# Delta-net inversion with two heads beside each other in one 128-column product, and 16 of 32 modulation row products moved to the first attention

## The reference, cut to what matters

```python
mod = jax.nn.silu(c) @ w_ada[layer] + b_ada[layer]            # 6 x 1024 numbers
sh1, sc1, gt1, sh2, sc2, gt2 = jnp.split(mod, 6, axis=-1)
A = where(strict, einsum('id,jd->ij', kb, kc) * decay, 0.0)   # for a chunk and head
t_inv = triangular_solve(A + eye, eye, lower=True, unit_diagonal=True)
W = t_inv @ (kb * exp(Gcum));  U = t_inv @ (vc * bc)
v_new = U - W @ S;  S = S * gt + kt.T @ v_new                 # from chunk to chunk
```

## Time and profile before

| what | us |
|---|---|
| runs | 1801.17, 1801.20, 1801.35; median 1801.2 |
| span of the profiled execution | 1798.0 |
| outside the span, against the median | 3.2 |
| first attention, tiles 23 on | about 149 to 244 |
| inversion, first product to the end of the last level's updates | 255.05 to 403.4 |
| apply of the last round, read-out and norm up to the second phase's end | to 419.5 |

### The profile page before, as it was taken

The page is one execution under the profiler, slowest core; times in us unless marked ns, Lnnn a source line. Parts: engine busy times, 40 slices in busy tenths (PEclk is TensorE's granted clock), DMA queues, the critical chain, the costliest instruction groups (busy, mean ns, idle before and its releaser), DMA issues.

```text
span 1798.0 us, 34944 instructions
## 1 busy us (share of the span) xinstructions
PE 1751.7 (97%) x11968; PEld 1581.6 (88%) x11968; DVE 1300.8 (72%) x2596; ACT 1053.4 (59%) x2118; POOL 163.3 (9%) x136
## 2 busy tenths in 40 slices
PE   7999999999999999999999999999999999999998
PEld 1878789999999988888899999999899899999997
DVE  3787456667889979766766666666686767878887
ACT  2545553343666689766655555555657666766666
POOL 0000004410284420000000000000010000010000
PEclk9999999999999999999999999999999999999999
DMA  8433223234455421355555555555444534455553
GB/s 298 183 105 106 80 86 114 75 105 170 149 197 175 166 93 37 117 193 191 189 197 186 187 187 186 187 186 187 152 176 142 198 130 141 165 181 186 184 186 129
DMA packets 77273, 283.34 MB, mean 158 GB/s; under 512 B 8576, under 2 KB 8576, under 8 KB 76928
## 3 DMA queue, kind: packets, MB, share of 16 engines
q1 hardware_dynamic: 77184, 282.16, 45.6%
HBM read 281.08 MB, written 1.05 MB: 157 GB/s over the span
## 4 chain that ended last, share of the span: by engine, by line
PE 83%; DVE 10%; ACT 4%; issue 1%; POOL 1%; DMA 1%; PEld 0%; PEldq 0%; ACTq 0%; SPq 0%; DVEq 0%
PE banks L867 19%; PE banks L855 16%; PE banks L946 10%; PE banks L455 7%; PE banks L1102 7%; PE banks L1126 3%; PE banks L646 2%; PE banks L797 2%; PE banks L627 2%; DVE split L2331 2%; DVE arena L2327 2%; PE banks L423 1%; PE banks L635 1%; PE banks L960 1%; PE banks L1062 1%
## 5 line engine op out<-in xcount | busy, mean ns | idle before, releaser
L1447 ACT ACTIVATE split<-arena 128x512 fp32r<-128x512 f32 x492 | 309.0, 629 | 135.1 <-PE banks L855 76.9
L855 PEld LDWEIGHTS banks<-split 128*128 128x128 f32 x2880 | 355.4, 192 | 10.6 <-DVE split L2257 3.1
L867 PE MATMUL banks<-split 128*128 128x512 f32 x1536 | 361.9, 390 | 1.0 <-issue 1.0
L855 PE MATMUL banks<-split 128*128 128x256 f32 x2880 | 358.7, 283 | 3.2 <-DVE split L2257 2.3
L2349 DVE TENSOR_TENSOR split<-arena,split 128x512 fp32r<-128x512 f32 x396 | 270.7, 690 | 105.5 <-ACT split L1447 99.7
L867 PEld LDWEIGHTS banks<-split 128*128 128x128 f32 x1536 | 283.8, 188 | 57.3 <-issue 1.4
L1425 ACT ACTIVATE split<-arena 128x512 fp32r<-128x512 f32 x312 | 194.5, 627 | 112.1 <-PE banks L1102 52.8
L946 PE MATMUL banks<-split 128*128 128x256 f32 x1728 | 216.8, 287 | 4.3 <-DVE split L2427 3.9
L946 PEld LDWEIGHTS banks<-split 128*128 128x128 f32 x1728 | 211.9, 194 | 7.2 <-issue 6.0
L2404 DVE TENSOR_TENSOR split<-arena,split 128x512 fp32r<-128x512 f32 x180 | 123.1, 694 | 65.3 <-ACT split L1425 63.8
L455 PEld LDWEIGHTS banks<-split 128*128 128x128 f32 (+1 forms) x936 | 132.4, 192 | 28.5 <-issue 13.8
(11 more groups left out here) (412 smaller groups left out, 2418.2 us busy)
## 6 DMA issues: line engine op xcount, KB each, us to landing
arena<-wstream SPq DMA_DIRECT2D x525, 512.0 KB, 3.3
arena<-x_t SPq DMA_DIRECT2D x1, 2048.0 KB, 12.4
arena<-matsa SPq DMA_DIRECT2D x1, 1234.0 KB, 6.3
out_t<-arena SPq DMA_DIRECT2D x4, 256.0 KB, 2.0
arena<-mats SPq DMA_DIRECT2D x1, 576.0 KB, 8.1
arena<-crow SPq DMA_DIRECT2D x1, 512.0 KB, 7.1
arena<-rows SPq DMA_DIRECT2D x1, 512.0 KB, 4.1
arena<-mats SPq DMA_DIRECT2D x1, 449.0 KB, 4.2
```

The source lines that it names most:

```text
L855: mm = pe.matmul(ps[:, 4 + b, 0:S], w_parts[:, c, (2 * m + half) % 4, P * k:P * k + P], h_parts[:, e, 4 * half + k, :], start=(half == 0 a ...
L867: mm = pe.matmul(ps[:, 2 * tt + half, :], g_parts[:, e, j % 2, P * tt:P * tt + P], w_parts[:, c, (2 * m + half) % 4, :], start=(first and ...
L1447: act.activation(w_parts[:, 0, (2 * m + half) % 4, :], ring[:, peer_slot(m), 512 * half:512 * half + 512], ACT.Copy).then_inc(sem["w_hi"], 1)
```

## The change

It packs the half of `Z` that a level works on, and the keys it needs, so that two heads lie side by side in one 128x128 block. One product with 128 columns then serves two heads; what comes out between different heads is zeroed by a mask of blocks (`blocks`), in place of the mask of a single head. So each level has two products, two turns and two products of 128 columns for each direction. ACT gets new work: `pack_keys` gathers the keys of the next level, `keep_half` carries over the half of `Z` that a level doesn't change, and at level 6 it copies the products in two pieces. `Z` alternates between `Z1` and `Z2`, so the products wait for DVE's subtraction and for both ACT copies. The copy of `T` halves to 128x256. `first_inverse` becomes two DVE instructions of 128x256.

16 of the 32 `mod_tail` now stand in the first attention, each behind `both_lo` of a tile (the first two behind tiles 23 and 24), and their weight tiles alternate with tiles 23 to 38 in `wstream` and in the ring. 2 stay before the inversion and 14 within it. Two waits (`gain3_in`, `lam_exp`) go.

```diff
@@ -44,6 +44,9 @@
...
+FIRST_TAIL, EARLY_TAILS = 23, 16
+in_at = lambda t: N_WIN + t + min(max(t - FIRST_TAIL, 0), EARLY_TAILS)
+tail_at = lambda a: N_WIN + FIRST_TAIL + 2 * a + 1 if a < EARLY_TAILS else N_ADA2 + a
@@ -233,9 +236,9 @@
...
         at = buf("at", 4, 4, P)
-        PAIR = ("E", "A0", "A1", "Z0", "Z1", "T", "KB", "VB", "KT", "S", "wt", "uu")
-        pair = [{n: buf(f"{n}{d}", 4, P) for n in PAIR} for d in range(2)]
-        yp = [buf(f"yp{d}", 256) for d in range(2)]
+        PAIR = ("E", "A0", "A1", "Z0", "Z1", "Z2", "AP", "T", "KB", "VB", "KT", "S", "wt", "uu")
+        pair = [{n: buf(f"{n}{d}", 2 if n == "T" else 4, P) for n in PAIR} for d in range(2)]
@@ -326,7 +329,35 @@
...
+        flat = lambda v: v.rearrange("p a b -> p (a b)")
         parts = lambda v, l, q: v.rearrange("p (b q s) -> p b q s", q=2, s=2 ** l)[:, :, q, :]
+        def inverse_at(d, l):
+            return flat(pair[d]["Z0" if l == 1 else "Z1" if l % 2 == 0 else "Z2"])
+        def half_at(d, l, q):
+            return inverse_at(d, l)[:, 256 * q:256 * q + 256]
+        def next_half(d, l, q):
+            v = inverse_at(d, l + 1)
+            if l == 6:
+                return parts(v, 6, q)
+            return v.rearrange("p (x g q s) -> p x g q s", x=2, q=2, s=2 ** l)[:, :, :, q, :].rearrange("p x g s -> p g x s")
+        def as_next(v, l):
+            return v.rearrange("p (g s) -> p g s", s=64) if l == 6 else v.rearrange("p (g x s) -> p g x s", x=2, s=2 ** l)
+        def as_packed(v, l):
+            return v.rearrange("p (g s) -> p g s", s=2 ** l)
+        def keys_at(d, l):
+            return flat(pair[d]["AP"])[:, 256 * (l % 2):256 * (l % 2) + 256]
         block = ctx.enter_context(nc.Block())
@@ -363,16 +394,21 @@
...
-                    sp.wait_ge(sem["in_lo"], 2 * (n - RING - N_WIN) + 2)
+                    if n - RING in in_tiles:
+                        sp.wait_ge(sem["in_lo"], 2 * in_tiles[n - RING] + 2)
+                    else:
+                        sp.wait_ge(sem["tail_done"], early_tails[n - RING] + 1)
                     sp.dma_start(tile_at(n), wstream[n]).then_inc(loaded[n % RING], 16)
+            in_tiles = {in_at(t): t for t in range(39)}
+            early_tails = {tail_at(a): a for a in range(EARLY_TAILS)}
@@ -616,40 +652,38 @@
                 mm.then_inc(sem["m_turned"], 1)
             def level_products(n, l, d):
-                z, a = pair[d][f"Z{n % 2}"], pair[d][f"A{n % 2}"]
                 if l == 1:
                     if n == 0 and d == 1:
                         pe.wait_ge(sem["proj_free"], 4 + 39)
                     pe.wait_ge(sem["z1_ready"], step_at(n, d))
                 else:
                     pe.wait_ge(sem["z_ready"], level_at(n, l - 1, d))
-                for h in range(4):
-                    mm = pe.matmul(ps[:, d, 64 * h:64 * h + 64], a[:, h, :], parts(z[:, h, :], l, 1 - d), start=True, stop=True)
+                    pe.wait_ge(sem["z_kept"], level_at(n, l - 1, d))
+                pe.wait_ge(sem["keys_packed"], level_at(n, l, d))
+                for j in range(2):
+                    c = slice(P * j, P * j + P)
+                    mm = pe.matmul(ps[:, d, c], keys_at(d, l)[:, c], half_at(d, l, 1 - d)[:, c], start=True, stop=True)
                 mm.then_inc(sem["y_done"], 1)
                 if l == 1:
                     if n:
                         pe.wait_ge(sem["wu_ready"], step_at(n - 1, d))
                     else:
                         pe.wait_ge(sem["tok_ready"], 3 + d)
-                for h in range(4):
-                    mm = pe.transpose(ps[:, 2 + d, P * h:P * h + P], z[:, h, :], ident)
+                for j in range(2):
+                    mm = pe.transpose(ps[:, 2 + d, P * j:P * j + P], half_at(d, l, d)[:, P * j:P * j + P], ident)
                 mm.then_inc(sem["z_turned"], 1)
             def level_update(n, l, d):
-                if l < 6:
-                    pe.wait_ge(sem["y_out"], 10 * n + 2 * (l - 1) + d + 1)
-                else:
-                    pe.wait_ge(sem["y_last"], step_at(n, d))
+                pe.wait_ge(sem["y_out"], level_at(n, l, d))
                 pe.wait_ge(sem["t_ready"], level_at(n, l, d))
-                r = slice(0, P) if l < 6 else slice(64 * d, 64 * d + 64)
-                for h in range(4):
-                    mm = pe.matmul(ps[:, d, 256 + 64 * h:320 + 64 * h], pair[d]["T"][r, h, :], yp[d][r, 64 * h:64 * h + 64],
-                                   start=True, stop=True)
+                for j in range(2):
+                    mm = pe.matmul(ps[:, d, 256 + P * j:256 + P * j + P], pair[d]["T"][:, j, :], yp[d][:, j, :], start=True, stop=True)
                 mm.then_inc(sem["p_done"], 1)
             def apply_inverse(n, d):
-                b, z = pair[d], pair[d][f"Z{n % 2}"]
+                b, z = pair[d], pair[d]["Z2"]
                 pe.wait_ge(sem["z_ready"], level_at(n, 6, d))
+                pe.wait_ge(sem["z_kept"], level_at(n, 6, d))
                 pe.wait_ge(sem["kv_ready"], step_at(n, d))
                 if n == 0:
                     pe.wait_ge(sem["tok_ready"], 8)
@@ -1340,15 +1374,36 @@
...
+            def pack_keys(n, l, d):
+                if l == 1:
+                    act.wait_ge(*((sem["mask_ready"], d + 1) if n == 0 else (sem["a_beta"], step_at(n - 1, d))))
+                act.activation(as_packed(keys_at(d, l), l), parts(flat(pair[d][f"A{n % 2}"]), l, d), ACT.Copy).then_inc(sem["keys_packed"], 1)
+            def keep_half(n, l, d):
+                act.wait_ge(*((sem["z1_ready"], step_at(n, d)) if l == 1 else (sem["z_ready"], level_at(n, l - 1, d))))
+                act.activation(next_half(d, l, d), as_next(half_at(d, l, d), l), ACT.Copy).then_inc(sem["z_kept"], 1)
+            for d in range(2):
+                pack_keys(0, 1, d)
             for n in range(4):
                 for l in range(1, 7):
                     for d in range(2):
+                        keep_half(n, l, d)
+                    for d in range(2):
                         if l == 6:
                             act.wait_ge(sem["y_done"], level_at(n, l, d))
-                            act.activation(yp[d].rearrange("p (a b) -> p a b", a=4)[64 * d:64 * d + 64], ps[64 * d:64 * d + 64, d, 0:256].rearrange("p (a b) -> p a b", a=4), ACT.Copy).then_inc(sem["y_last"], 1)
+                            for q in range(2):
+                                r = slice(64 * q, 64 * q + 64)
+                                o = act.activation(yp[d][r, :, r], bank(d, 2, P)[r, :, r], ACT.Copy)
+                            o.then_inc(sem["y_out"], 1)
                         act.wait_ge(sem["z_turned"], level_at(n, l, d))
-                        act.activation(pair[d]["T"].rearrange("p a b -> p (a b)"), ps[:, 2 + d, :], ACT.Copy).then_inc(
-                            sem["t_ready"], 1)
+                        act.activation(flat(pair[d]["T"]), ps[:, 2 + d, 0:256], ACT.Copy).then_inc(sem["t_ready"], 1)
+                    for d in range(2):
+                        if l < 6:
+                            pack_keys(n, l + 1, d)
+                        elif n < 3:
+                            pack_keys(n + 1, 1, d)
                     if n == 0 and l in (2, 4):
                         tok_move(2 + l)
@@ -1956,6 +2010,18 @@
...
+            def mod_tail(a):
+                n = tail_at(a)
+                dve.wait_ge(loaded[n % RING], 16 * (n // RING + 1))
+                dve.scalar_tensor_tensor(tile_at(n), tile_at(n), 1.0, crow, ALU.mult, ALU.mult,
+                                         accum_out=modT[:, 16 + a, 0:1]).then_inc(sem["tail_done" if a < EARLY_TAILS else "tiles_done"], 1)
+            def lo_and_tail(t):
+                both_lo(t)
+                if FIRST_TAIL <= t < FIRST_TAIL + EARLY_TAILS:
+                    mod_tail(t - FIRST_TAIL)
             dve.wait_ge(sem["late_in"], 48)
@@ -2046,7 +2107,11 @@
...
                 dve.wait_ge(sem["m_turned"], step_at(n, d))
-                dve.tensor_tensor(pair[d][f"Z{n % 2}"], bc(ident, 1, 4), bank(4 + d, 4, P), ALU.subtract).then_inc(sem["z1_ready"], 1)
+                for q in range(2):
+                    o = dve.tensor_tensor(half_at(d, 1, q).rearrange("p (a b s) -> p a b s", a=4, s=2),
+                                          bc(ident.rearrange("p (b q s) -> p b q s", q=2, s=2)[:, :, q, :], 1, 4),
@@ -2099,22 +2164,21 @@
...
-            dve.sem_inc(sem["tiles_done"], 1)
-            TAILS = ((2, 1, 1, 1, 2, 3), (1, 0, 1, 0, 2, 2), (1, 1, 0, 0, 2, 2), (1, 1, 1, 1, 2, 2))
+            dve.sem_inc(sem["tiles_done"], 1 + EARLY_TAILS)
+            TAILS = ((1, 1, 0, 0, 1, 2), (0, 0, 0, 1, 1, 2), (0, 0, 0, 0, 1, 2), (0, 0, 0, 0, 0, 2))
             for n in range(4):
                 for l in range(1, 7):
                     for d in range(2):
                         if l < 6:
                             dve.wait_ge(sem["y_done"], level_at(n, l, d))
```

(10 more changed lines are left out.)

52 lines of the change are left out of this document (25 added, 27 removed).

## The result

| kernel | runs, median | ratio to before, 95% interval |
|---|---|---|
| before | 1801.28 (1801.17 to 1804.38) | |
| the change | 1770.33 (1766.74 to 1771.14) | 0.9824, 0.981 to 0.9838 |

The change takes 31 us off. The forecast was 35 off, 1766.4, with a range of 1757 to 1778. The median of before holds one run more here (1804.38) than where 1801.2 was given. The runs of the changed kernel spread over 4.4 us, of which more is said at the end. A run's time holds 1.8 us outside the span here, where the profiled execution of before had 3.2.

A forecast was written before the change was run, and what follows sets the result against it. PE was taken to bound the inversion and first attention, with the chain through DVE and ACT taking over in the inversion. 37.6 us gained there less 2.8 lost in the attention gave 34.8 off 1801.2: 1766.4, range 1757 to 1778.

The forecast's parts named there:

- PE bounds before, and its load falls by half: Inversion: PE busy 151.3 of 152 us; its load in a level falls by 2.2 us to 2.2.
- A bare level takes 2.7 us, bound by the chain through ACT and DVE: Inversion level without other work: 2.7 us instead of 4.4, with PE idle some 0.5 of it.
- Levels with other work: Inversion levels with added PE or DVE work: for example 4.36 with eight products, 3.5 with eight turns, 8.2 for level 1.
- A row product costs DVE 1.14: One `mod_tail` on DVE takes 1.14 us from start to start; 16 moved into the attention cost 18 us of DVE.
- Attention loses 2.8: First attention: moved `mod_tail` delay the scores at two places by 1.9 and 0.8 us; 2.8 lost, bounds none to 8.
- What follows keeps its distance: Behind the inversion: state, norm and branches are unchanged and follow at the old distance.
- The time outside the span is unchanged: Whole run: the 3.2 us between profiled span and median stay, so 34.8 comes off the median.
- DMA costs nothing: First attention: weight loads start at least 5 us before ACT wants them and take 3.3 us, so cost nothing.
- That PE stays the bound: Inversion rival: handovers overlap better than added, up to the whole 53 us go, total 1753; chance 0.07.
- Dear short runs on ACT: Inversion rival: short-run copies cost 0.84 instead of 0.42 us, total 1779 to 1782; chance 0.18, shared with handovers adding up.
- The clock in the inversion: Inversion rival: PE's idle gaps lower its clock and the kernel gets slower, 1826 us; chance 0.03.
- the first rival: Inversion: PE stays the bound, up to 53 us go, total worked as 1801.2 - 51 + 2.8 = 1753; chance 0.07.

The follow-up runs named there:

- the kernel with the short row products: Against the kernel with both moves: the inversion's 14 row products cut to their first 64 of 1024 columns; 1760.31 us.
- the first experiment: Against the changed kernel: the attention's row products issued behind the next group's logits and maxima instead of ahead of them; 1764.87 us, ratio 0.9791.
- the first part alone: Against the changed kernel: two heads side by side kept, no row products in the attention, old weight order and table of places; 1781.91 us, ratio 0.9887.
- its form with other places: Against the first part alone: its 30 row products moved, mostly behind level 6 and the last 8 behind the inversion's end; 1779.12 us, ratio 0.9877.
- the kernel with both moves: Against the changed kernel: attention's row products behind logits and maxima, and 3 of the inversion's behind level 6 of every round; 1761.51 us, ratio 0.9786.
- the second part alone: Against the kernel before: 16 of 32 row products moved into the attention, inversion still in 64-column products; 1806.43 us, ratio 1.0025.
- 64 columns: Against the changed kernel: each 128-column product of the inversion's levels issued as two of 64 columns; 1801.52 us, ratio 1.0007.
- one copy more: Against the changed kernel: an extra unread 128x128 ScalarE copy ahead of each of the 48 keep_half copies; 1771.47 us, ratio 0.984.

## Why the prediction held

- **PE bounds before, and its load falls by half.** Held: PE's idle time rose from 0.7 to 7.8 us. With the old width back, the time is back at 1801.5.
- **A bare level takes 2.7 us, bound by the chain through ACT and DVE.** Held: 2.70 in round 0. The way there was not all right: I had `keep_half` of direction 1 ahead of `T` making 2.63 into 2.7, and it has 0.3 us of slack.
- **Levels with other work.** 4.36 forecast, 4.34 measured, once in round 1 and four times in round 3; level 1, 8.2 forecast, measured 8.19 to 8.27. The rounds came out at 19.4, 30.4, 29.5 and 28.6 for 20.1, 29.7, 29.2 and 28.5. That the sum is within 0.5 us is in part luck: level 6 of round 0 took 3.8 for 4.4, and two levels with a row product took 1.2 more than forecast.
- **A row product costs DVE 1.14.** Mis-sized beside GpSimd: 2.0 to 2.2. It gave level 5 of round 1 0.7 us more and level 6 of round 2 0.6. Gain of the inversion: 37.1, forecast 37.6.
- **Attention loses 2.8.** The two waits measured 1.85 and 0.80 for 1.9 and 0.8. The term lacked the clock behind the first one, 1.5 us. Measured 4.7, within the bounds of 0 to 8.
- **What follows keeps its distance.** Wrong by 2.5 us: the last subtraction is 32.4 earlier, the span's end 29.9. At one place behind the phase, PE waits 1.18 and 0.92 us in the kernel before, in the change and in the kernel with the short row products, the same to a hundredth. The 48 pieces behind these waits take 6.02 us in before and in the last, and in the change the first 39 take 6.43:

```profile
1403.11 0.72 PE L1028 MATMUL banks<-arena 64*128 64x128 f32 x8 [1.18 <-ACT arena L1641]
1404.75 1.10 PE L1028 MATMUL banks<-arena 64*128 64x128 f32 x8 [0.92 <-DVE arena L2604]
1405.78 6.43 PE L980 MATMUL banks<-split 128*128 128x256 f32 x39
```

```profile
1393.42 0.71 PE L1028 MATMUL banks<-arena 64*128 64x128 f32 x8 [1.18 <-ACT arena L1641]
1395.06 1.10 PE L1028 MATMUL banks<-arena 64*128 64x128 f32 x8 [0.92 <-DVE arena L2607]
1396.09 6.02 PE L980 MATMUL banks<-split 128*128 128x256 f32 x48
```

  The clock fell in the one (0.75 from 1407 to 1412 us) and not in the other, some 1.5 us. It fell at this place in eight of the eleven kernels here. The rest, 1.0 us, was lost near 1293 us, where PE waits for GpSimd in the change (first row) and not before (second row); why GpSimd was late there stays open:

```profile
1293.39 0.70 PE L842 MATMUL banks<-arena 128*128 128x256 f32 x2 [1.23 <-POOL arena L2909]
```

```profile
1324.24 1.28 PE L808 MATMUL banks<-arena 128*128 128x256 f32 x4
```

- **The time outside the span is unchanged.** Wrong: 1.8 us for 3.2 in the profiled executions. In the runs of before it lies between 1.7 and 3.1. These 1.4 us came to the forecast's help and were not foreseen.
- **DMA costs nothing.** Held: the first experiment has all its traffic and none of the loss.
- **The rivals.** That PE stays the bound: its idle time of 7.8 us excludes it. Dear short runs on ACT: 419 ns excludes it. Of the lines of 16 bytes in "SBUF — State Buffer" of the Trainium skill, section "Door 1: The DMA port swizzle", this trace shows at most a small price: some 25 ns on 417 in the one level with runs of 8 bytes. The clock in the inversion: 1.00 in the change (259 to 373 us). But it was the right thing to fear: I had taken the 3.4 us of the earlier trace rows as the kind of wait that it needs, and it fell behind waits of 0.72 to 2.54.

Two sums of the prediction are off by a little: round 2 adds up to 29.3, not 29.2, and the first rival takes 51 us off where its working gives 53, so that it would stand at 1751.

In sum, with the terms as measured: 37.1 for 37.6, 4.7 for 2.8 and 2.5 for 0 make 29.9 for 34.8, by the spans of the two profiled executions. With the 1.4 us outside them it is 31.3 between these two runs; the medians are 31.0 apart.

## What to carry to other kernels

A term for PE that idles after a change is not only the wait but the wait and what the clock may do behind it. When another engine's work is placed beside a chain, ask where the chain waits for something else, and put it there: 14 row products, 12 of them behind the rounds' last levels, cost nothing, and 16 more spread over all levels 0.9 us each, 0.2 of it by the clock. And a move that frees an engine is worth what the bound of that stretch makes of it: the same move lost 5 us before the products were widened and gained 12 with them.

## What the hardware showed that I had not expected

**A row product and GpSimd exclude each other.** In the inversions of the change, of the first part alone, of its form with other places and of the kernel with both moves stand 88 row products. The 59 that are clear of GpSimd take 1.21 to 1.23 us each; of the 29 that overlap it, 17 take 1.4 to 2.3. What decides is who begins first. In the rows of level 5 of round 1 above, GpSimd began at 305.56, and the row product of 305.64 ends where 1.04 of GpSimd and its own 1.1 have passed one after the other. In round 0 of the change it was the other way round, the row product first (DVE, then POOL):

```profile
284.32 1.22 DVE L2018 SCALAR_TENSOR_TENSOR arena<-arena 128x1024 f32<-128x1024 f32 x1
```

```profile
284.67 1.77 POOL L2861 TENSOR_TENSOR arena<-arena 128x512 f32<-128x512 f32 x1 [3.35 <-PE banks L697]
286.40 1.04 POOL L2862 TENSOR_TENSOR arena<-arena 128x512 f32<-128x512 f32 x1
```

The row product keeps its 1.22, and GpSimd's instruction takes 1.77 for 1.04. DVE's instructions with one input from PSUM are not slowed: in the change's inversion the 14 of 128x512 that overlap GpSimd take 0.68 each, as those clear of it do. Nor do they slow it: one took 0.68 at 305.04, with GpSimd busy from 304.33 to 305.61 at the 1.28 that this instruction has elsewhere too. The Trainium skill's "SBUF — State Buffer", section "SBUF: two separate sides", has this rule: a DVE instruction with two inputs in SBUF and a GpSimd instruction that reads SBUF lock a shared pair of ports for their whole length, and the one that comes later stands. The traces agree with what it says of time: two inputs from SBUF, the whole length, and the later one stands; of ports they show nothing. With it, the 2.05 us of row products in the trace of before could have been read for what they were, and the 0.7 us of level 5 put into the sum.

**The clock falls behind waits that look harmless, and not always.** The wait of 1.85 us at the second group's scores was followed by a fall in the change, in the second part alone and in the experiments with 64 columns and one copy more, and by none in that with row products behind level 6 (clock 1.00 from 159 to 165 us). The wait of 0.80 was followed by a fall in the second part alone and in that last one, and not in the change. The wait of 2.35 in the inversion was harmless in the change and cost over 1 us in the first experiment (2.36 there). Behind the wait of 0.72 at the attention's end, which every kernel here has, it fell in two kernels, the first part alone and its form with other places, and in no other, before included. The falls priced here cost from some 1.1 us (level 6 of round 1 with one copy more) to 3.2 (the attention's end of the first part alone). What decides it, with the same instructions ahead of it, no run here shows: the five waits of 1.85 end within 0.17 us of each other (158.06 to 158.23 us), and the one without a fall is the earliest by 0.05. The mean clock goes with how runs of one kernel spread, though not strictly: the four of the change have mean clocks of 0.992, 0.993, 0.995 and 0.992 beside 1769.91, 1770.74, 1766.74 and 1771.14 us.
